# Attention's values taken for 512 queries at once, and VectorE's sorting put ahead of its wait for stores, in a two-layer diffusion backbone

## The chip, the cores and the metric

The kernel runs on one core of one Trainium2 chip, as one program. The metric is the device time of one execution in microseconds; of several executions the median counts. Profiles show one execution each.

## The reference, cut to what matters

A latent stream of 512 tokens and a context of 256 tokens, both 1024 wide, pass two layers. Layer 0 mixes with a bidirectional gated recurrence, layer 1 with latent attention of 16 heads; behind each stands a mixture of 16 experts, where each expert chooses its tokens. All in float32. What the change touches:

```
def attend(q, k, v):                      # 512 queries, 768 keys (latent + context), 16 heads
    s = jnp.einsum('bqhd,bkhd->bhqk', q, k).astype(jnp.float32) * ATTN_SCALE
    p = jax.nn.softmax(s, axis=-1).astype(v.dtype)
    return jnp.einsum('bhqk,bkhd->bqhd', p, v)

def ec_moe(h, router, w_up, w_down):
    cap = CAPACITY_FACTOR * T // N_EXPERTS               # 64 of 512 tokens, 32 of 256
    aff = jax.nn.softmax((h @ router).astype(jnp.float32), axis=-1)
    gate, idx = lax.top_k(jnp.swapaxes(aff, 1, 2), cap)
    xg = h[bidx, idx]
    up = jnp.einsum('becd,edf->becf', xg, w_up)
    hid = jax.nn.silu(up[..., :D_EXPERT]) * up[..., D_EXPERT:]
    y = jnp.einsum('becf,efd->becd', hid, w_down) * gate[..., None].astype(h.dtype)
    return jnp.zeros_like(h).at[bidx, idx].add(y)
```

A head has 96 numbers for query and key and 64 for the value. An expert's weights are 12 MB (8 chunks of `up`, 4 of `down`, 1 MB each); each layer reads 192 chunks.

## The kernel before, in words

The program is written engine by engine, with semaphores by hand; each engine runs its instructions in the order of the text. SP issues the loads of weights in the order of one list (`chunks`, L415) into buffers of 1 MB: `ring`, slots 0 to 7, and `ring_x`, slots 8 to 18, which lie over memory that the mixers use before. Each load waits until its slot is free (`used[slot]`, counted up by the last matmul that reads it, or by VectorE where a whole area is handed over), so one load that waits holds all later ones. `free_at` holds planning numbers that choose the slot of each chunk.

**Choosing tokens** (`choose`, L1404, VectorE; `turn_choice`, L638, TensorE). VectorE makes the affinities, TensorE turns them, VectorE takes 64 places in 8 rounds of maximum, index and replacement (L1425 to L1428), TensorE turns the lists, VectorE forms the indices `idx_t` and releases GpSimd's first gather (L1737). Between affinities and sorting stands `open_experts` (L1381): it waits until the rows of `stream` and `normed` have been stored, fills `mod_a`, `mod_b` and a zero area, and marks slots of `ring_x` as free. `residual_norm` and GpSimd's `stores` run ahead of it.

**Attention** (L817, L1150, L1582, L1767) runs in a loop of 4 groups of 4 heads. A group starts with projections: `kv_project` for 6 tiles of 128 tokens, with `turn_keys`, then `q_project` for 4 tiles with `turn_queries`; VectorE splits each result in two parts. Then come 16 units of one head and 128 queries, by pairs of heads, and in a pair by query tile. For unit u the engines do:

- TensorE: `scores(u)` into one half of `wide` (needs the exponential of u - 2), then `turn_probs(u - 3)` into `turned`; after every second unit `values(w)` for the pair of units before, into `duo`.
- VectorE: reciprocal of u - 1 (L1634, needs its exponential), maximum of u (L1638), its share of copying turned probabilities of u - 3 to `PT` (L1646).
- ScalarE: its share of that copy (L1168), then the exponential (L1176, needs the maximum) into `prob`, which has `LAG` = 3 places.
- GpSimd: probabilities times reciprocal (L1770).

`values(w)` is 12 calls, each with 64 columns of `V` as the stationary operand and 128 queries as the moving one; two heads go to the two halves of the partitions. `PT` holds two pairs of units, so its copies wait for the `values` of two pairs earlier (`s_av`). At a pair's end VectorE copies 512 queries from `duo` to `OT`. The float32 matmuls stand in the profile as two records each.

**After attention** `out_project` (L577) applies `w_o`; five small turnings ahead of it mark the slots of `uq` and `ukv` free. The weights of attention lie in `ring`: `mla_in` 0 to 2, `uq` 3 to 5, `ukv` 6 and 7, `w_o` 0 to 3. Slots 15 to 18 (`EARLY`) are marked free at the end of attention.

## Time and profile before

| | us |
|---|---|
| median of 3 runs | 1939.77 (1939.23 to 1940.5) |
| profiled execution | 1941.09, its span 1939.4 |
| TensorE busy (matmuls) | 1678.6, 87% of the span |
| VectorE, ScalarE, GpSimd busy | 623.4, 487.6, 202.4 |
| DMA | 528.6 MB, mean 273 GB/s |
| layer 0's experts | 409.7 to about 960 |
| attention's groups | scores of the first from 1079.5; ends at 1126.5, 1198.0, 1269.1, 1341.5: 71.5 each |
| first expert's matmuls of layer 1 | 1440.07; first of its buffers reloaded at 1443.8 |
| first gather, layer 0 and layer 1, until it has landed | 8.5 and 6.3 |
| TensorE's clock under 1 in attention | 1080 to 1090, 1158 to 1161.5, 1295 to 1305 |

The span is that of one execution on the chip; the profiled execution's own time is 1.7 us longer. Engine times are sums of instructions, so a busy TensorE says nothing of its pace: the clock (PEclk) is 1 at 2.4 GHz and 0.5 at 1.2 GHz. The chain of waits, followed back from the last instruction, gives 61% of the span to TensorE and 20% to SP's queue of weight loads (L415).

### The profile page before, as it was taken

Reading aid. Unit: us, or ns where it says so; the run is one execution under the profiler, and the core shown is the slowest. Engines: PE = TensorE matmul, PEld = TensorE weight load, DVE = VectorE, ACT = ScalarE, POOL = GpSimd, SP = SyncE. Lnnn points to the kernel's source line nnn. Section 1 sums busy time; section 2 is a strip of 40 time slices with the busy share of each in tenths; the row PEclk is TensorE's granted clock in tenths of the full one; section 3 lists DMA queues with packets and bytes.
Section 4 is the critical chain, followed back from the end, with each engine's and each line's share of the span. In section 5 each row is a group of like instructions: output and inputs, shape, how many; then the busy total and the mean of one; then the engine's idle time right before and its main releaser. Section 6 shows DMA issues by size and latency. Waiting matters only on the chain.

```text
span 1939.4 us, 22466 instructions
## 1 busy us (share of the span) xinstructions
PE 1678.6 (87%) x9117; PEld 787.8 (41%) x9117; DVE 623.4 (32%) x1333; ACT 487.6 (25%) x847; POOL 202.4 (10%) x199
## 2 busy tenths in 40 slices
PE   4999979759999999999969989899949978787874
PEld 2677634323333333333245767767423322222221
DVE  4666643321121222212134555553341111111111
ACT  5678741201110111111141434533210000000001
POOL 1000010000000000000000323413000000000000
PEclk8999989879999999999979899989959999999997
DMA  9454451799999999999741000002579999999997
GB/s 363 161 194 155 174 201 70 274 399 355 390 402 385 402 380 402 397 389 373 247 178 66 1 1 0 0 0 116 213 288 404 398 397 413 399 413 397 413 397 294
DMA packets 92082, 528.59 MB, mean 273 GB/s; under 512 B 11875, under 2 KB 20176, under 8 KB 36448
## 3 DMA queue, kind: packets, MB, share of 16 engines
q1 hardware_dynamic: 80704, 489.84, 63.0%
q0 software_dynamic: 11296, 37.58, 7.2%
q8 instruction: 61, 1.00, 0.2%
q14 instruction: 21, 0.17, 0.0%
HBM read 504.21 MB, written 23.17 MB: 272 GB/s over the span
## 4 chain that ended last, share of the span: by engine, by line
PE 61%; SPq 20%; ACT 6%; DVE 5%; DMA 5%; issue 2%; DVEq 0%; ACTq 0%; POOLq 0%
SPq L415 20%; PE wide L680 14%; PE wide L593 7%; PE duo L720 6%; PE wide L688 6%; PE turned L465 6%; PE wide L538 5%; PE duo L730 3%; PE wide L881 2%; PE duo L904 2%; PE duo L826 2%; DMA sb_ring_x<-moe_w_down 1%; DMA sb_ring<-ada_w 1%; PE duo L845 1%; PE wide L791 1%
## 5 line engine op out<-in xcount | busy, mean ns | idle before, releaser
L680 PE MATMUL wide<-sb_ring_x,sb_xT 128*64 128x512 f32 x1136 | 267.4, 612 | 39.6 <-DMA sb_ring_x<-moe_w_up 38.6
L680 PE MATMUL wide<-sb_ring,sb_xT 128*64 128x512 f32 x912 | 213.0, 609 | 27.9 <-DMA sb_ring<-moe_w_up 26.2
L1466 DVE TENSOR_TENSOR sb_hid<-wide,sb_sg 128x512 f32<-128x512 f32 x32 | 22.1, 691 | 617.7 <-ACT sb_sg L1091 312.7
L1091 ACT ACTIVATE sb_sg<-wide 128x512 f32<-128x512 f32 x32 | 19.1, 598 | 674.9 <-PE wide L688 346.4
L680 PEld LDWEIGHTS wide<-sb_ring_x,sb_xT 128*64 128x64 f32 x1136 | 77.2, 140 | 215.7 <-issue 134.9
L720 PE MATMUL duo<-sb_ring_x,sb_hidT 128*64 128x512 f32 x592 | 138.5, 601 | 9.1 <-DMA sb_ring_x<-moe_w_down 9.0
L1758 POOL DMA_INDIRECT stream<-sb_ye,sb_idx_t x30 | 43.1, 1436 | 901.8 <-DVE sb_ye L1489 901.8
L680 PEld LDWEIGHTS wide<-sb_ring,sb_xT 128*64 128x64 f32 x912 | 62.6, 139 | 165.3 <-issue 109.3
L1770 POOL TENSOR_TENSOR sb_prob<-sb_prob,sb_asum 128x768 f32<-128x768 f32 x64 | 93.9, 1466 | 260.6 <-DVE sb_asum L1634 260.6
L593 PE MATMUL wide<-sb_ring,sb_areaY 128*128 128x512 f32 x192 | 85.5, 605 | 9.7 <-DVE sb_areaY L1365 9.7
L720 PE MATMUL duo<-sb_ring,sb_hidT 128*64 128x512 f32 x368 | 86.2, 601 | 6.0 <-DMA sb_ring<-moe_w_down 5.4
L1481 DVE SCALAR_TENSOR_TENSOR sb_ye<-duo,sb_gate_t,sb_gffn 64x512 f32<-64x512 f32 x30 | 22.3, 743 | 204.2 <-PE duo L730 103.7
L1111 ACT ACTIVATE sb_ye<-duo 64x512 f32<-64x512 f32 x30 | 17.8, 594 | 271.3 <-PE duo L730 146.9
L720 PEld LDWEIGHTS duo<-sb_ring_x,sb_hidT 128*64 128x64 f32 x592 | 38.2, 136 | 95.9 <-issue 67.2
L538 PE MATMUL wide<-sb_hT_hi,sb_w_hi 128*128 128x512 f32 (+1 forms) x256 | 70.1, 356 | 6.7 <-DVE sb_hT_lo L1304 6.7
L538 PE MATMUL wide<-sb_hT_lo,sb_w_hi 128*128 128x512 f32 (+1 forms) x256 | 67.4, 345 | 0.0
L538 PE MATMUL wide<-sb_hT_hi,sb_w_lo 128*128 128x512 f32 (+1 forms) x256 | 66.8, 343 | 0.0
L688 PE MATMUL wide<-sb_ring_x,sb_xT 128*32 128x512 f32 x568 | 65.6, 595 | 0.0
L1176 ACT ACTIVATE sb_prob<-wide,sb_asum 128x768 f32<-128x768 f32 x64 | 57.7, 901 | 30.5 <-DVE sb_asum L1638 30.4
L1638 DVE TENSOR_REDUCE sb_asum<-wide 128x1 f32<-128x768 f32 x64 | 60.7, 948 | 13.7 <-PE wide L882 13.6
L593 PEld LDWEIGHTS wide<-sb_ring,sb_areaY 128*128 128x128 f32 x192 | 37.0, 195 | 54.8 <-issue 44.9
L465 PE MATMUL turned<-sb_ident,sb_prob 128*128 128x128 f32 x384 | 54.9, 280 | 5.1 <-ACT sb_PT L1168 5.1
(302 smaller groups left out, 2388.3 us busy)
## 6 DMA issues: line engine op xcount, KB each, us to landing
sb_ring_x<-moe_w_up SPq DMA_DIRECT2D x142, 1024.0 KB, 13.0
sb_ring<-moe_w_up SPq DMA_DIRECT2D x114, 1024.0 KB, 14.3
sb_ring_x<-moe_w_down SPq DMA_DIRECT2D x80, 1024.0 KB, 15.9
sb_ring<-moe_w_down SPq DMA_DIRECT2D x48, 1024.0 KB, 13.2
sb_ring<-ada_w SPq DMA_DIRECT2D x40, 1024.0 KB, 6.7
sb_ring<-lru_w_in SPq DMA_DIRECT2D x8, 1024.0 KB, 9.1
sb_ring_x<-ada_w SPq DMA_DIRECT2D x8, 1024.0 KB, 7.8
sb_ring<-lru_w_out SPq DMA_DIRECT2D x4, 1024.0 KB, 6.5
```

The costliest lines, as they stand in the source:

```text
L415: sp.dma_start(dst, src).then_inc(landed[slot], 16)
L465: return nc.tensor.transpose(dst, src, ident[0:n, 0:n])
L538: ins = mm(wide[:, b, :] if i == 0 else wide[:, b + 1, 0:TC], w[:, p % 2, k, :], seg(h[:, k, :], i), start=k == 0 and n == 0, stop=k == KD ...
L593: ins = mm(wide[:, b + n, :], lhs(k, t), w[:, n * BANK:(n + 1) * BANK], start=k == 0, stop=k == KD - 1)
L680: ins = mm(wide[n * CAPL:(n + 1) * CAPL, s, :], xT[:, k, 0:CAPL], w[:, at:at + BANK], start=k == 0, stop=k == KD - 1)
L688: ins = mm(wide[n * CAPC:(n + 1) * CAPC, 2, :], xT[:, k, CAPL:M], w[:, n * BANK:(n + 1) * BANK], start=k == 0, stop=k == KD - 1)
L720: ins = mm(lat[n * CAPL:(n + 1) * CAPL, :], hidT[:, 2 * (c % 2) + r, h * CAPL:(h + 1) * CAPL], w[:, r, n * BANK:(n + 1) * BANK], start=c = ...
L730: ins = mm(both[at:at + CAPC, :], hidT_c[:, 2 * (c % 2) + r, h * CAPC:(h + 1) * CAPC], w[:, r, n * BANK:(n + 1) * BANK], start=c == 0, sto ...
L1176: fn(prob[:, u % LAG, :], wide[:, b:b + 2, :].rearrange("p a n -> p (a n)")[:, 0:T], ACT.Exp, bias=asum[:, 0, u % 4:u % 4 + 1], accum_out= ...
L1638: v.tensor_reduce(asum[:, 0, u % 4:u % 4 + 1], wide[:, b:b + 2, :].rearrange("p a n -> p (a n)")[:, 0:T], AX_X, ALU.max, negate=True).then ...
L1758: pool.indirect_dma_start(out=stream, out_offset=bass.IndirectOffsetOnAxis(ap=idx_t[0:M, e:e + 1], axis=0), in_=(ye if e < E - 1 else xg)[ ...
L1770: g_.tensor_tensor(prob[:, u % LAG, :], prob[:, u % LAG, :], asum[:, 2, u % 4:u % 4 + 1].to_broadcast([P, T]), ALU.mult).then_inc(s_pn, 1)
```

## The change

1. `values(pair)` takes 512 queries of two heads in one call, twice in a group: after turning unit 8, and after the last unit. Units go head by head. The turned probabilities of a whole head are kept: head number modulo 3 picks one of three places, two in slots 0 to 2 of `ring`, the third in `PT`, now [128, 6, 512]. A copy waits on `s_av` at the first unit of a head only.
2. The four loops over groups are written out, with constants in the waits. The next group's first `kv_project` stands ahead of a group's last `values`.
3. `w_o` lies in slots 6, 7, 3 and 4; `uq` and `ukv` are freed by matmuls of the last group; slots 0 to 2 are opened with `EARLY`. The five small turnings are gone.
4. The waits for stores and the marks move into the sorting (`open_buffers`; after round 4 in layer 0, after round 1 in layer 1); the fills of `open_experts` move behind the release of the first gather. TensorE gets a wait for them ahead of layer 1's first rows.

```
+    W_O = (6, 7, 3, 4)
+    PT_SLOTS = (0, 1, 2)
     for j in range(4):
-        chunk(("w_o", j), j)
+        chunk(("w_o", j), W_O[j])
     opened(range(RING, NCH))
+    opened(PT_SLOTS)
     for slot in range(NCH):
-        free_at[slot] = now + (2 if slot < 4 else 1 if slot < RING else 0 if slot in EARLY else 3)
+        free_at[slot] = now + (1 if slot in EARLY or slot in PT_SLOTS else 2 if slot in W_O else 3 if slot >= RING else 0)
...
-            ("prob", [P, LAG, T], F32), ("PT", [P, 2, 2, TT, P], F32), ("asum", [P, 3, 8], F32))
+            ("prob", [P, LAG, T], F32), ("PT", [P, TT, TL], F32), ("asum", [P, 3, 8], F32))
...
+        def turned_probs(head):
+
+            if head % 3 == 2:
+                return PT[:]
+            two = ring[:, 0:3, :].rearrange("p a b -> p (a b)")
+            return two[:, head % 3 * TT * TL:(head % 3 + 1) * TT * TL].rearrange("p (k n) -> p k n", k=TT)
...
+                if lay == 1:
+                    pe.wait_ge(s_ye[1], 1)
                 turn_rows(0, None)
...
-            with pe.Fori(0, NG) as g:
+            for g in range(NG):
...
-                kv_project(0)
+                if g == 0:
+                    kv_project(g, 0)
...
-                def values(w):
-
-                    pe.wait_ge(s_PTa, g * 16 + (2 * w + 3))
-                    pe.wait_ge(s_PTd, g * 16 + (2 * w + 3))
-                    _, t, pair, _ = unit(2 * w)
+                def values(pair):
+
+                    pe.wait_ge(s_PTa, g * 16 + (8 * pair + 9))
+                    pe.wait_ge(s_PTd, g * 16 + (8 * pair + 9))
                     for k in range(TT):
                         for hh in range(2):
-                            ins = mm(duo[hh * VD:(hh + 1) * VD, pair, t * P:(t + 1) * P], V[:, k, 2 * pair + hh, :],
-                                     PT[:, w % 2, hh, k, :], start=k == 0, stop=k == TT - 1)
+                            h = 2 * pair + hh
+                            ins = mm(duo[hh * VD:(hh + 1) * VD, pair, :], V[:, k, h, :], turned_probs(HG * g + h)[:, k, :],
+                                     start=k == 0, stop=k == TT - 1)
                     ins.then_inc(s_av, 1)
...
                         turn_probs(u - LAG)
-                        if (u - LAG) % 2 and u - LAG >= 3:
-                            values((u - LAG) // 2 - 1)
-                values(U // 2 - 1)
+                        if u - LAG == 2 * TLT:
+                            values(0)
+                if g + 1 < NG:
+                    kv_project(g + 1, 0)
+                values(1)
...
-            for n, name in enumerate([("uq", j) for j in range(KQ)] + [("ukv", j) for j in range(KKV)]):
-                turn(duo[0:32, 1, 32 * n:32 * n + 32], ident[0:32, 0:32]).then_inc(used[place[name][0]], 1)
...
-                        w, hh = divmod(u - LAG, 2)
+                        h, t = divmod(u - LAG, TLT)
                         act.wait_ge(s_ptr, g * 32 + (2 * (u - LAG) + 1))
-                        if hh == 0 and w >= 2:
-
-                            act.wait_ge(s_av, g * 8 + (w - 1))
+                        if t == 0 and HG * g + h >= 3:
+
+                            act.wait_ge(s_av, (HG * g + h - 3) // 2 + 1)
...
-            def open_experts(lay):
-
-                M, s = CAP[lay], 2 * lay + 1
+            def open_buffers(lay):
 
                 dve.wait_ge(s_st[lay], 16 * FFT[lay])
                 dve.wait_ge(s_nst[lay], 16 * FFT[lay])
+                for j in range(RING, NCH):
+                    if lay == 0 or j not in EARLY:
+                        mark(used[j], 1)
+
+            def open_experts(lay):
+
+                M, s = CAP[lay], 2 * lay + 1
...
-                open_experts(lay)
                 dve.wait_ge(s_afft, lay + 1)
...
+                    if r == (CAPL // 16 - 1 if lay == 0 else 0):
+                        open_buffers(lay)
...
                 mark(s_sel, 1)
+                open_experts(lay)
...
-            for j in EARLY:
+            for j in PT_SLOTS + EARLY:
                 mark(used[j], 1)
```

VectorE in `choose(0)`, before. `sb_aff` are the affinities, `sb_marks` the marks that open slots, `sb_affT` the turned affinities.

```order
L1418 TENSOR_TENSOR sb_aff<-sb_aff,sb_mx 128x2x16 x3
L1392 COPY sb_mod_a<-sb_cols 128x8x64
L1392 COPY sb_mod_b<-sb_cols 128x8x64
L1392 COPY sb_mod_a<-sb_cols 128x8x32
L1392 COPY sb_mod_b<-sb_cols 128x8x32
L1395 MEMSET sb_hid_c 64x512
L1195 MEMSET sb_marks 128x1 x12
L1422 COPY sb_affT<-turned 48x256
```

The same place after, and under it the middle of the sorting.

```order
L1436 TENSOR_TENSOR sb_aff<-sb_aff,sb_mx 128x2x16 x3
L1439 COPY sb_affT<-turned 48x256
L1442 MAX sb_lists<-sb_affT 48x8
L1443 MAX_INDEX sb_top_i<-sb_lists,sb_affT 48x8
L1445 MATCH_REPLACE sb_affT<-sb_lists,sb_affT 48x256
```

```order
L1442 MAX sb_lists<-sb_affT 48x8
L1443 MAX_INDEX sb_top_i<-sb_lists,sb_affT 48x8
L1445 MATCH_REPLACE sb_affT<-sb_lists,sb_affT 48x256
L1211 MEMSET sb_marks 128x1 x11
L1442 MAX sb_lists<-sb_affT 48x8
L1443 MAX_INDEX sb_top_i<-sb_lists,sb_affT 48x8
```

The four copies and the zeroing are gone from ahead of the sorting, and the marks, whose first waits for the stores, stand behind the fourth round.

TensorE at the end of a group, before: the scores of unit 15 and what follows them. `sb_prob` are probabilities to be turned, `sb_V` the values, L817 the loop's own end.

```order
L882 MATMUL wide<-sb_k_hi,sb_q_lo 128x256
L465 MATMUL turned<-sb_ident,sb_prob 128x128 x12
L904 MATMUL duo<-sb_PT,sb_V 64x128 x12
L465 MATMUL turned<-sb_ident,sb_prob 128x128 x12
L904 MATMUL duo<-sb_PT,sb_V 64x128 x12
L899 REGISTER_ALU
L904 MATMUL duo<-sb_PT,sb_V 64x128 x12
L817 REGISTER_ALU
L817 COMPARE_AND_BRANCH
```

The end of the second group, after.

```order
L898 MATMUL wide<-sb_k_hi,sb_q_lo 128x256
L470 MATMUL turned<-sb_ident,sb_prob 128x128 x24
L833 MATMUL duo<-sb_ring,sb_ckvT 128x512 x2
L920 MATMUL duo<-sb_ring,sb_V 64x512 x12
L833 MATMUL duo<-sb_ring,sb_ckvT 128x512 x2
L470 MATMUL turned<-sb_ident,sb_ktok 96x128 x4
L833 MATMUL duo<-sb_ring,sb_ckvT 128x512 x2
L470 MATMUL turned<-sb_ident,sb_ktok 96x128 x4
```

The three last `values` of 128 queries have become one of 512, the four turnings stand alone behind the scores, and the next group's first projection (L833) has moved ahead of `values`.

TensorE in the middle of a group, before: a turning with the `values` behind it, and the next unit.

```order
L465 MATMUL turned<-sb_ident,sb_prob 128x128 x6
L904 MATMUL duo<-sb_PT,sb_V 64x128 x12
L876 REGISTER_ALU
L881 MATMUL wide<-sb_k_hi,sb_q_hi 128x512
L882 MATMUL wide<-sb_k_hi,sb_q_hi 128x256
L881 MATMUL wide<-sb_k_lo,sb_q_hi 128x512
L882 MATMUL wide<-sb_k_lo,sb_q_hi 128x256
L881 MATMUL wide<-sb_k_hi,sb_q_lo 128x512
L882 MATMUL wide<-sb_k_hi,sb_q_lo 128x256
L465 MATMUL turned<-sb_ident,sb_prob 128x128 x6
```

The same after, from the unit ahead of `values(0)`.

```order
L898 MATMUL wide<-sb_k_hi,sb_q_lo 128x256
L470 MATMUL turned<-sb_ident,sb_prob 128x128 x6
L920 MATMUL duo<-sb_ring,sb_V 64x512 x12
L897 MATMUL wide<-sb_k_hi,sb_q_hi 128x512
L898 MATMUL wide<-sb_k_hi,sb_q_hi 128x256
L897 MATMUL wide<-sb_k_lo,sb_q_hi 128x512
L898 MATMUL wide<-sb_k_lo,sb_q_hi 128x256
L897 MATMUL wide<-sb_k_hi,sb_q_lo 128x512
L898 MATMUL wide<-sb_k_hi,sb_q_lo 128x256
L470 MATMUL turned<-sb_ident,sb_prob 128x128 x6
```

`values` stands once between two units, with four times the columns, and no longer behind every second one.

## Rows read from the trace of the kernel before

**Rows 1.** The page: two lines of 40 equal slices of the span, busy tenths.

```profile
PE   4999979759999999999969989899949978787874
...
DMA  9454451799999999999741000002579999999997
```

**Rows 2.** The chain of waits: start, length (us), engine, tile, line, count of records.

```profile
1242.42 1.46 PE duo L904 x24
...
1273.13 1.72 PE duo L826 x4
...
1475.27 7.02 PE duo L720 x32
```

**Rows 3.** Instructions in order of time, third group: start, us, instruction [idle <-releaser].

```profile
1231.10 0.94 DVE L1638 TENSOR_REDUCE sb_asum<-wide 128x1 f32<-128x768 f32 x1
...
1232.15 0.90 ACT L1176 ACTIVATE sb_prob<-wide,sb_asum 128x768 f32<-128x768 f32 x1 [0.68 <-DVE sb_asum L1638]
...
1233.17 0.16 DVE L1634 RECIPROCAL sb_asum<-sb_asum 128x1 f32<-128x1 f32 x1 [0.80 <-ACT sb_prob L1176]
...
1233.19 0.50 PE L881 MATMUL wide<-sb_k_hi,sb_q_hi 96*128 96x512 f32 x1 [0.17 <-ACT sb_prob L1176]
1233.25 0.94 DVE L1638 TENSOR_REDUCE sb_asum<-wide 128x1 f32<-128x768 f32 x1
```

**Rows 4.** The same view, later in that group.

```profile
1243.81 0.50 PE L881 MATMUL wide<-sb_k_hi,sb_q_hi 96*128 96x512 f32 x1
...
1245.18 0.96 DVE L1638 TENSOR_REDUCE sb_asum<-wide 128x1 f32<-128x768 f32 x1 [0.67 <-PE wide L882]
...
1250.26 0.96 DVE L1638 TENSOR_REDUCE sb_asum<-wide 128x1 f32<-128x768 f32 x1 [0.67 <-PE wide L882]
```

**Rows 5.** The same view, start and end of that group.

```profile
1224.83 0.94 DVE L1638 TENSOR_REDUCE sb_asum<-wide 128x1 f32<-128x768 f32 x1
...
1261.51 0.90 ACT L1176 ACTIVATE sb_prob<-wide,sb_asum 128x768 f32<-128x768 f32 x1
...
1266.22 2.84 PE L904 MATMUL duo<-sb_PT,sb_V 128*64 128x128 f32 x48
...
1269.23 0.69 DVE L1627 COPY sb_OT<-duo 128x512 f32 x1 [2.48 <-PE duo L904]
...
1272.53 0.60 PE L465 MATMUL turned<-sb_ident,sb_ktok 128*96 128x128 f32 x4
```

**Rows 6.** Stretches: start:end, length, busy PE, PEld, DVE, ACT, POOL, PEclk, DMA share, GB/s.

```profile
438.00:442.00 4.00, 3.67 (x14) 2.26 (x16) 0.18 (x1) 0.87 (x2) 0.00 (x0) 0.57 1.04 357
...
1080.00:1090.00 10.00, 9.85 (x33) 7.95 (x32) 5.31 (x9) 4.63 (x10) 4.40 (x3) 0.50 0.00 1
...
1224.00:1270.00 46.00, 42.31 (x385) 35.71 (x384) 24.34 (x51) 26.12 (x50) 23.46 (x16) 1.00 0.00 0
```

**Rows 7.** Instructions in order of time, where layer 0 chooses its tokens.

```profile
374.28 0.40 PE L465 MATMUL turned<-sb_ident,sb_aff 128*48 128x128 f32 x2 [0.35 <-DVE sb_aff L1418]
380.88 0.43 DVE L1392 COPY sb_mod_a<-sb_cols 128x512 f32<-128x512 f32 x1 [6.66 <-DMA normed<-sb_units]
...
382.83 0.42 DVE L1422 COPY sb_affT<-turned 48x256 f32<-48x256 f32 x1
...
384.77 0.42 DVE L1425 MAX8 sb_lists<-sb_affT 48x8 f32<-48x256 f32 x1
...
397.89 0.98 POOL L1737 DMA_INDIRECT sb_xg<-normed,sb_idx_t  x1 [15.43 <-DVE sb_marks L1195]
```

**Rows 8.** Waits of TensorE from 420 to 960 us: us in total, times, longest.

```profile
PE turned L465 <- DVE sb_xT L1461: 4.3, 1, 4.3
```

**Rows 9.** Layer 1's choice, in order of time; below, one stretch as in rows 6.

```profile
1414.10 0.62 PE L465 MATMUL turned<-sb_ident,sb_aff 128*48 128x128 f32 x2 [1.91 <-DVE sb_aff L1418]
...
1416.03 0.42 DVE L1422 COPY sb_affT<-turned 48x256 f32<-48x256 f32 x1
...
1436.00:1440.00 4.00, 1.97 (x8) 1.56 (x8) 1.65 (x4) 0.00 (x0) 0.63 (x1) 0.50 0.02 3
```

More of the change, by code:

```diff
@@ L826, in kv_project @@
                         ins = mm(duo[:, t % 2, :], ckvT[:, k, t * P:(t + 1) * P],
-                                 ring_at(("ukv", k))[:, bass.ds(g * BANK, BANK)], start=k == 0, stop=k == KKV - 1)
+                                 ring_at(("ukv", k))[:, g * BANK:(g + 1) * BANK], start=k == 0, stop=k == KKV - 1)
+                        if g == NG - 1 and t == TT - 1 and k == 0:
+                            ins.then_inc(used[place["ukv", 0][0]], 1)
                     ins.then_inc(s_kv, 1)
@@ L870, in scores @@
                 def scores(u):
[L871 removed]
+                    h, t = divmod(u, TLT)
                     if h == 0:
@@ L1149, in _ @@
                 fn(mx[:, 3, t:t + 1], mx[:, 1, t:t + 1], ACT.Sqrt, bias=eps[:, 0:1], scale=1.0 / KVL).then_inc(s_mzs, 1)
-            with act.Fori(0, NG) as g:
+            for g in range(NG):
                 for t in range(TT):
@@ L1399, in open_experts @@
                 mark(s_ye[lay], 1)
-                for j in range(RING, NCH):
-                    if lay == 0 or j not in EARLY:
-                        mark(used[j], 1)
             def choose(lay):
@@ L1581, in _ @@
             loop_chain = Chain(dve, s_dloop)
-            with dve.Fori(0, NG) as g:
+            for g in range(NG):
                 loop_chain.n = g * TLT
@@ L1766, in _ @@
             pool.dma_start(ropes[:], rope.rearrange("(t p) i f -> p t i f", p=P)).then_inc(s_rope, 16)
-            with pool.Fori(0, NG) as g:
+            for g in range(NG):
                 for u in range(HG * TLT):
```

34 lines of the change are left out of this document (18 added, 16 removed).

## The prediction, made before the changed kernel ran

> **What bounds the kernel now.** I read the page's slices first. TensorE is at 7 to 9 tenths almost everywhere, but the DMA line splits the run in three: full DMA and full TensorE through layer 0's experts (slices 9 to 19), no DMA at all through attention (slices 23 to 27), full DMA and a TensorE at 7 to 8 tenths in layer 1's experts at the end [rows 1]. So a microsecond counts differently by stage.
>
> Layer 0's experts are TensorE's: from 420 to 960 us TensorE's one wait over 1 us was for VectorE, 4.3 us, and none was for a DMA [rows 8]. What starts them sooner ends them sooner. Layer 1's experts wait for weights, but their first weights do not: all 19 buffers are full and the DMA engines idle (share 0.02) from 1436 to 1440 us, waiting for the first expert's matmuls to free a buffer [rows 9]. So the last stage too begins where TensorE begins it, and every shift before it comes out whole.
>
> Attention is a row of 4 groups of 16 units (one head, 128 queries). In a unit TensorE computes scores, VectorE their maximum, ScalarE the exponentials, VectorE the reciprocal, GpSimd the product, and TensorE turns the probabilities of three units earlier. Two limits show. In the middle of a group, maxima stand 5.08 us apart for two units, VectorE idle behind TensorE for 0.67 us [rows 4]: that is TensorE's limit, two units of scores and turning and one `values` of 1.46 us [rows 2]. At a group's start there is no `values`, and then another limit shows: maximum at 1231.10, exponential at 1232.15, reciprocal at 1233.17, next maximum at 1233.25 [rows 3]. VectorE does not start a maximum before the reciprocal of the unit before, so VectorE and ScalarE take turns, 2.15 us for each unit, whatever TensorE does. That chain lies only 0.39 us a unit under today's 2.54.
>
> **The change, part by part.**
>
> (a) `values` for 512 queries. Before, a pair of heads takes 4 calls of 24 records with 128 columns: 4 x 1.46 = 5.84 us, and a gap of about 0.17 us ahead of each. After it is one call of 24 records with 512 columns. The trace has that shape in the expert's `down`: 32 records in 7.02 us, 0.219 each [rows 2], so 24 take 5.27 us. TensorE saves 0.57 us and three gaps for each of 8 pairs: about 1.1 us each, 9 in all. But where it is spent decides. TensorE's work a unit without `values` is (5.08 - 1.46 - 0.17) / 2 = 1.72 us, less than the chain's 2.15. So the loop runs at 2.15 a unit, and the 5.27 us come as one lump in the middle and one at the end.
>
> The Trainium skill ("TensorE: Matmul & The Clock Gate", Part 1, "Wait — 56ns, not 53.3ns?") gives each matmul a fixed cost of about 2.5 ns on top of its columns. The rows show more here: 60.8 ns for a record of 128 columns against 219 / 4 = 54.9, so 8 ns for each of three records saved. By the page's figure the eight pairs would save 1.4 us of matmul time in place of 4.6. Neither reaches the end of the kernel if the chain sets the pace.
>
> Middle of a group, counted from its first maximum (`wide` has two halves, so scores of unit u start 1.04 us after the exponential of unit u - 2 [rows 3]): maximum 11 at 11 x 2.15 = 23.5 (the first steps are a little shorter); maximum 9 at 19.2, its exponential at 20.25, scores 11 at 21.3, then turning, `values(0)` from 23.2 to 28.4. Scores 12 start there, and their maximum comes 1.37 later, as in [rows 4]: 29.8 instead of 25.7. The stall is 4.1 us. Three more units and 1.05 give exponential 15 at 37.3. Before, that is 1261.51 - 1224.83 = 36.7 [rows 5]. So all that the loop won (about 3.5 us) and the saved gaps are spent by one stall: **+0.6 us a group**.
>
> End of a group. Before: from exponential 15 to the end of the last two `values`, which take 2.84 us, 1269.06 - 1261.51 = 7.55 us [rows 5]. After: the last turning starts about 3.4 us after exponential 15 (nearly as now: GpSimd's product and ScalarE's copies of units 13 to 15 set it) and takes 0.57; then `kv_project` of the next group, 1.72 [rows 2], covering the wait for the last copies; then 5.27: 10.96. That is +3.4 us, of which the next group gets something back: before, its first key turning starts 3.47 us after the end of `values` [rows 5]; after, the second projection waits for the copy to `OT` (0.17 + 0.69 + 0.05 us) and takes 1.72, so 2.6: -0.8. The last group has no projection to cover: +2.4. Sum over the groups: 4 x 0.65 + 3 x (3.4 - 0.8) + 2.4 = **+12.8, with rounding 13 us**. Bounds: the stall may be 1 us shorter or longer in each group, so 9 to 17.
>
> (b) Loops written out. The waits of the loops compare with registers; written out they compare with constants. Nothing in the trace prices that alone. A wait of one semaphore inside the loop releases its instruction in 0.03 us, as outside; the exponential that waits for two comes 0.11 us after its maximum ends (1231.10 + 0.94 to 1232.15). If the second wait gets free, 0.08 us for 52 units is 4.2 us; if not, 0. A loss is possible through instruction fetching, but the DMA engines are idle there, so 0.5 at most. I take **-1** (range -4.2 to +0.5), nearer to nothing since a second wait stays.
>
> (c) TensorE's clock. The third group ran at full clock throughout; the first lost it from 1080 to 1090 us [rows 6] (the fourth for as long, the second for some 3 us: the table of the profile), right after a stretch in which TensorE only turned queries and idled. In layer 0, five microseconds of idling and turning, 433 to 438, were followed by 438 to 442 at clock 0.57 [rows 6]. After the change each group ends with about 6 us (from scores 15 to the next matmul that isn't a turning) where TensorE turns four times 0.57 us and idles between; now it is 2.3 us. I expect 1.2 GHz there in about three of four groups, over some 3.4 us of dense matmuls as in layer 0, which costs half of it, 1.7 us: **+5** (range 0 to 14: no dip, or twice that length in every group).
>
> (d) VectorE sorts first in layer 0. TensorE has turned the affinities at 374.68, and VectorE waits 6.66 us for the stores, fills `mod_a`, `mod_b` and `hid_c`, and copies `affT` at 382.83 [rows 7]. After, the copy starts at about 374.75. A round takes 384.77 - 382.83 - 0.45 = 1.49 us, so four are done at 381.2; the stores had landed at 380.88, so the wait is then free, and the 11 marks cost 0.25. The choice, and the gather at 397.89, come 8.08 - 0.25 = 7.8 us earlier. The filling (1.8 us) now runs behind the gather, which takes 8.5 us (table); `ada_read(4)` and its turning move back by 1.8 us and still end under it. SP's 11 loads of `ring_x` are let go at 381.3 instead of 382.7. **-7.8 us** (-5.5 if the gather, now deeper inside the burst of weight loads, takes 2 us longer; -8.5).
>
> (e) The same in layer 1. No store was waited for there; the fills stood between the turned affinities (1414.72) and the copy at 1416.03 [rows 9]: -1.3, and 7 marks inside the sorting +0.15: **-1.1**. TensorE's new wait for `s_ye` has nothing queued that could go, and the fills (1.9 us) lie under a gather of 6.3 us (table).
>
> (f) Slots. `w_o` sits in 6, 7, 3, 4 and loads while the last group runs, one expert chunk (slot 5) too, seven more at the end of attention; before it was w_o's last chunk and eight. Then SP waits in order for slots 3, 4, 6, 7: three of those loads start up to 16 us later than now. They fit: 3 x 2.6 us more before the last seven, whose end moves to about 1436.5 on the old scale, while the first buffer is freed at 1443.8 now (table) and at 1442.7 with (e). Idle DMA from 1436 to 1440 [rows 9] is the cover; if it were gone, up to 3 us. Counted 0. The five small turnings ahead of `out_project` go: **-0.3**.
>
> Sum: +12.8 - 1 + 5 - 7.8 - 1.1 - 0.3 = +7.6 us by the middles; with the rounding of (a) up, **+8**. The profiled execution took 1941.1 us (span 1939.4), 1.3 over the median of 1939.8; against the median I forecast **1948**.
>
> **The rivals.**
>
> *The clock holds.* All as above without (c): 1939.8 + 3 = 1942.8, +-2. For it: two of four groups come through their present idle stretch undisturbed or nearly. Against it: that stretch gets twice as long.
>
> *Not slower: the lump costs nothing in the middle.* If the stall of 4.1 us were covered in each group, 16.4 us go: 1948 - 16.4 = 1931.6. It decides at a stall of about 2 us, that is if VectorE and ScalarE had two units in hand when `values(0)` starts. Against it: scores start only 1.04 us after an exponential [rows 3], so they have under two. A stronger reading, that TensorE is the bound and its saved 9 us come out whole, gives 1939.8 - 9 - 9.2 = 1921.6; [rows 3] speak against it.
>
> *The clock oscillates in the loop.* At 1.2 GHz TensorE needs 9.85 of 10 us for what it does at a slower pace [rows 6]; a unit then takes about 3.0 us in place of 2.15, so each stretch of 10 us costs some 3 us; one or two more of them in each group but those that have one: about +8, 1956. The Trainium skill says the same of kernels that cycle PSUM banks ("TensorE: Matmul & The Clock Gate", "A second HAM failure mode: psum-queue depth-cycling"): idling briefly between groups of matmuls, often enough, makes the clock swing. Against it: the starts of groups, which already run chain-bound for 10 us, kept full clock in two groups of four or lost it for 3 us only.
>
> *Layer 0 gives nothing back.* If weights, not TensorE, set layer 0's experts, (d) is lost: 1955.8. [rows 8] speak against it, though the DMA share is as full there [rows 1].
>
> **How the numbers follow.** A difference under 0.2% (3.9 us) is about what a measurement of this kernel can't tell from none. Forecast (1944 to 1953): 0.50, slower. Clock holds: 0.25, of it 0.08 slower and 0.17 within. Lump covered, or TensorE the bound: 0.10, faster. Clock oscillates: 0.10, slower. Layer 0's gain lost: 0.05, slower. So faster 0.10, within 0.17, slower 0.73. The range leaves out the faster case and the outer half of the slow ones and takes in the bounds of (a) to (d) about their middles: 1939 to 1957.
>
> **What would show it.** `values` at 24 records in 5.3 us. Maxima 2.1 to 2.2 us apart through most of a group and one step of 6.3 us after unit 11. About 11 us from a group's last exponential to the end of its `values`; groups of 74 to 76 us where they are 71.5 now. Clock 0.5 inside `kv_project` and `values(1)`. Layer 0's gather at about 390, its experts 7.8 us earlier up to 960. DMA idle just ahead of layer 1's first expert. I am wrong if the 6.3 us step isn't there, or if the loop's pace is well under 2.1 us (then (b) was too small), or if layer 0's experts end no sooner.

## The result, and the profile after

The changed kernel took **1945.4 us** (median of 14, 1943.4 to 1949.0) against 1940.95 (14 runs) for the kernel before on the same chip: ratio 1.0023 (1.0015 to 1.0031), some 4.5 us slower. The forecast was 1948, slower. The executions of one kernel spread over some 6 to 8 us here; the profiled one of after is the slowest of its 14 (1949.0, span 1947.3), that of before is at its median. So totals are compared by the ratios, and the traces by stage.

| stage, us | before | after | difference | forecast |
|---|---|---|---|---|
| start to affinities turned, layer 0 | 374.28 | 375.20 | +0.9 | 0 |
| from there to the first gather | 23.61 | 15.75 | -7.9 | -7.8 |
| gather to VectorE's first copy of projected keys, where attention begins | 658.06 | 659.32 | +1.3 | 0 |
| from there to the last copy to `OT` | 285.69 | 297.69 | +12.0 | +16.8 |
| last copy to `OT` to the end of the span | 597.76 | 599.34 | +1.6 | -1.4 |

Attention holds the loss, as forecast, though less. The chain of waits of after, in the first group and at the end of the last (start, length, engine, tile, line, count):

```profile
1097.99 5.30 PE duo L920 x24
...
1104.58 0.97 DVE sb_asum L1658
...
1115.68 1.72 PE duo L833 x4
1117.40 5.33 PE duo L920 x24
...
1340.96 6.98 PE duo L920 x24
```

`values(0)` takes 5.30 us and is followed by scores and a maximum; at the end `kv_project` and `values(1)` stand in a row on the chain. In the last group `values(1)` takes 6.98 us, at a clock that had fallen (below). VectorE's instructions around the middle lump, in order of time:

```profile
1098.13 0.94 DVE L1658 TENSOR_REDUCE sb_asum<-wide 128x1 f32<-128x768 f32 x1
...
1104.58 0.96 DVE L1658 TENSOR_REDUCE sb_asum<-wide 128x1 f32<-128x768 f32 x1 [4.28 <-PE wide L898]
...
1122.75 0.69 DVE L1647 COPY sb_OT<-duo 128x512 f32<-128x512 f32 x1 [6.60 <-PE duo L920]
```

One step of 6.45 us, VectorE idle for 4.28 of it, where [rows 4] have two units in 5.08. All other maxima stand 2.08 apart, but for one step of 2.6 near the start of each of the last three groups. The last row answers to the copy in [rows 5]: VectorE waits 6.60 us for it, 2.48 before. Stretches at the ends of the four groups (columns as in [rows 6]):

```profile
1113.00:1121.00 8.00, 7.01 (x34) 3.27 (x36) 1.17 (x3) 1.48 (x3) 1.47 (x1) 1.00 0.00 0
1186.00:1194.00 8.00, 6.81 (x26) 3.94 (x28) 1.33 (x4) 2.25 (x5) 1.70 (x2) 0.79 0.01 2
1262.00:1270.00 8.00, 7.48 (x30) 4.09 (x32) 0.90 (x3) 1.22 (x3) 1.28 (x1) 0.79 0.01 2
1338.00:1346.00 8.00, 7.04 (x25) 2.98 (x25) 0.85 (x2) 1.20 (x2) 0.28 (x1) 0.61 0.00 0
```

The granted clock (third number from the end) falls in the ends of the last three groups, not of the first. From the last maximum to the copy to `OT` it takes 11.92, 13.13, 13.13 and 13.39 us; before, 8.80 in all four.

Layer 0's choice, the rows that answer to [rows 7]:

```profile
375.64 0.42 DVE L1439 COPY sb_affT<-turned 48x256 f32<-48x256 f32 x1 [0.50 <-PE turned L470]
...
382.08 0.24 DVE L1211 MEMSET sb_marks<- 128x1 f32 x10
...
390.95 1.24 POOL L1757 DMA_INDIRECT sb_xg<-normed,sb_idx_t  x1 [7.51 <-DVE sb_marks L1211]
```

The sort starts at once, and the wait for stores inside it costs under 0.1 us. From 420 to 960 us TensorE waits just as in [rows 8] (4.3 us, once). In layer 1 the stretch of [rows 9] looks otherwise. First the gather, from the chain of waits (6.33 us before), then two stretches:

```profile
1435.56 8.85 DMA sb_xg<-normed,sb_idx_t
```

```profile
1436.00:1440.00 4.00, 0.00 (x0) 0.00 (x0) 0.99 (x3) 0.00 (x0) 0.52 (x1) 0.50 1.01 422
...
1444.00:1448.00 4.00, 2.48 (x10) 1.86 (x12) 1.67 (x4) 0.00 (x0) 1.24 (x2) 0.50 0.07 29
```

The DMA engines are full while the gather runs, and idle only from 1444 on.

### The profile page after: what moved, and what is told of

Its sections match the earlier page's. It is cut to its first block, busy times and chain, and to the rows that moved or that the text cites. A ratio compares the mean times of both kernels' runs of the same rounds, so it can differ in the third digit from the quotient of the medians.

```text
span 1947.3 us, 20675 instructions
## 1 busy us (share of the span) xinstructions
PE 1683.1 (86%) x8536; PEld 758.4 (39%) x8536; DVE 620.8 (32%) x1336; ACT 481.4 (25%) x844; POOL 202.5 (10%) x199
## 4 chain that ended last, share of the span: by engine, by line
PE 58%; SPq 20%; ACT 8%; DVE 7%; DMA 4%; issue 2%; ACTq 0%; DVEq 0%; POOLq 0%
SPq L420 19%; PE wide L685 14%; PE wide L598 7%; PE duo L725 6%; PE wide L693 6%; PE wide L543 5%; PE turned L470 4%; PE duo L735 3%; DVE sb_asum L1658 2%; ACT sb_prob L1192 2%; PE duo L833 2%; PE duo L920 2%; DMA sb_ring<-moe_w_down 1%; DMA sb_ring<-ada_w 1%; PE duo L854 1%
## 5 line engine op out<-in xcount | busy, mean ns | idle before, releaser
L685 PE MATMUL wide<-sb_ring_x,sb_xT 128*64 128x512 f32 x1160 | 272.8, 613 | 34.9 <-DMA sb_ring_x<-moe_w_up 34.9
L725 PE MATMUL duo<-sb_ring_x,sb_hidT 128*64 128x512 f32 x568 | 132.9, 600 | 9.5 <-DMA sb_ring_x<-moe_w_down 9.3
L1778 POOL DMA_INDIRECT stream<-sb_ye,sb_idx_t x30 | 43.1, 1436 | 901.9 <-DVE sb_ye L1509 901.9
L725 PE MATMUL duo<-sb_ring,sb_hidT 128*64 128x512 f32 x392 | 92.0, 601 | 6.2 <-DMA sb_ring<-moe_w_down 5.8
L470 PE MATMUL turned<-sb_ident,sb_prob 128*128 128x128 f32 x384 | 59.3, 293 | 8.4 <-ACT sb_ring L1184 5.8
## 6 DMA issues: line engine op xcount, KB each, us to landing
sb_ring_x<-moe_w_down SPq DMA_DIRECT2D x75, 1024.0 KB, 14.3
```

Of the source, the lines that this page charges most:

```text
L470: return nc.tensor.transpose(dst, src, ident[0:n, 0:n])
L685: ins = mm(wide[n * CAPL:(n + 1) * CAPL, s, :], xT[:, k, 0:CAPL], w[:, at:at + BANK], start=k == 0, stop=k == KD - 1)
L725: ins = mm(lat[n * CAPL:(n + 1) * CAPL, :], hidT[:, 2 * (c % 2) + r, h * CAPL:(h + 1) * CAPL], w[:, r, n * BANK:(n + 1) * BANK], start=c = ...
L1778: pool.indirect_dma_start(out=stream, out_offset=bass.IndirectOffsetOnAxis(ap=idx_t[0:M, e:e + 1], axis=0), in_=(ye if e < E - 1 else xg)[ ...
```

## The experiments

All kernels were timed beside the kernel before; traces are of one execution each.

**The two halves of the change.** The kernel before with the sorting first:

```
+                    if r == (CAPL // 16 - 1 if lay == 0 else 0):
+                        open_buffers(lay)
...
                 mark(s_sel, 1)
+                open_experts(lay)
```

> The kernel before with part 4 alone (sorting ahead of the wait for stores, fills behind the gather's release). Theory A (layer 0 is TensorE's, layer 1's first expert sets the end): layer 0's gather 7.8 us earlier and all of it kept, layer 1's first gather 1.1 us earlier with the same 6.3 us latency, since the slots are those of before: 1940.9 - 8.9 = about 1932. Rival B (some of layer 0's gain is given back by the weight loads, as the profile of the changed kernel hints, where only 5.5 of 7.9 us were left at the start of attention): -6.5, 1934.5. Rival C (it gives nothing): 1941.

Measured: 1935.5, ratio 0.9973 (0.9964 to 0.9981), some 5 us less, nearest to rival B. Trace: layer 0's gather at 389.52 (-8.4), its first expert 8.1 sooner, attention 7.2 sooner; 0.5 us of each was there before the sort. Layer 1 gives nothing: its gather is issued 1.2 us sooner after the last copy to `OT` but takes 8.63 us instead of 6.33.

The changed kernel with the sorting as before (`open_experts` with its waits and marks ahead of the sort):

> The changed kernel without part 4. Theory A: attention costs 10 to 12 us and the later slots some 2 us more: +12 to +14 against before, about 1954. Rival (the two parts do not add, for example because attention hides behind something): within 5 us of before. With the first run it tells whether the parts add up to the measured +4.4.

Measured: 1955.1, ratio 1.0072 (1.0058 to 1.0086), +14.0. Attention in the trace: 297.40 us, +11.7. So attention costs and the sorting gives back, as the prediction had it. How much is less sure: the halves timed apart add up to 14.0 - 5.2 = 8.8 us and the whole is 4.5 over before, somewhat more than the intervals allow, while the traces differ the other way (+10.9 and -8.0 against +7.9). No run explains that.

**Loops written out** in the kernel before, nothing else:

```
-            with pe.Fori(0, NG) as g:
+            for g in range(NG):
```

> The kernel before with the four group loops written out and nothing else. Theory A (waits on registers cost 0.07 us a step in the chain of VectorE and ScalarE, which binds only the first units of a group here): maxima 2.08 apart in place of 2.15 at a group's start, middle unchanged at 5.08 for two: -1 to -3 us. Rival 1 (the 0.17 us gaps around values are register arithmetic too): 16 gaps a group go, -8 to -10 us. Rival 2 (loading more instructions costs): 0 to +3.

Measured: 1940.8, ratio 1.0000 (0.9989 to 1.0010). But the pace did change: where VectorE and ScalarE set it, maxima stand 2.08 apart in place of 2.07 to 2.16, and where TensorE sets it two units still take 5.08. In a group in which the clock did not fall, the first and the last maximum are 35.48 us apart (35.61 before), and from there to the last copy to `OT` it takes 8.52 (8.80): 0.4 us a group, 1.6 in all, less than this timing resolves (2 us either way).

**Is it the lump?** The changed kernel with one of six key tiles in `values(0)`:

```
+                    tiles = range(1) if pair == 0 else range(TT)
-                    for k in range(TT):
+                    for k in tiles:
```

> The changed kernel, but values(0), in the middle of each group, runs over one of its six key tiles, 4 records in place of 24; five sixths of the weighted sum for the first two heads of each group are left out. Theory A (one lump of 5.3 us stalls VectorE and ScalarE, since they have under two units in hand): the step after unit 11, 6.45 us in the changed kernel, becomes about 2.6 (1.72 + 0.88), 3.85 less in each of four groups, so 15 us less in all, about 1930; the other steps stay at 2.08. Rival B (the lump is paid for by work that TensorE has to do anyway, and steps behind it are then longer): under 4 us less in all, 1942 or more.

Measured: 1923.4, ratio 0.9913 (0.9900 to 0.9926), 22 us under the changed kernel. VectorE's row in the middle of the first group:

```profile
1098.87 0.96 DVE L1659 TENSOR_REDUCE sb_asum<-wide 128x1 f32<-128x768 f32 x1
```

It stands 2.14 after the one before (1096.73), not the 2.6 expected: what is left of `values(0)`, 1.0 us of TensorE, hides almost wholly, and the 4.3 us taken away came out as 4.31, 17.2 in four groups. Theory A holds. The other 4 to 5 us were not expected: here the clock did not fall in any group's end (11.91 us three times, 10.86 in the last).

**The same work in small pieces.** By head:

```
-                        if u - LAG == 2 * TLT:
-                            values(0)
+                        if u >= LAG + TLT:
+                            h, t = divmod(u - LAG - TLT, TLT)
+                            values(h, ((0, 1), (2,), (3, 4), (5,))[t])
...
-                values(1)
+                values(3, range(TT))
```

> The changed kernel, but the values are computed head by head and key tile by key tile: 1 or 2 of a head's 6 tiles behind each turning of the next head's units, and only the last head's 6 tiles, 2.64 us, stand at the group's end behind the next group's kv_project. The work is the same. Theory A (the lumps, not the work, cost the time): in the middle TensorE needs 1.72 + 0.66 = 2.38 us a unit for 8 units where VectorE and ScalarE want 2.08, so the stall of 4.37 us in a group becomes 2.4; the end gets 2.6 shorter; 4 x 4.6 = 18 us less than the changed kernel, about 1927, and below the kernel before by 14. From a group's first maximum to its second copy to OT 44.8 us in place of 49.5. Rival B (small pieces between scores let TensorE's clock fall or steps of 2.16 and 2.60 us don't even out, so each piece delays a maximum by its full length): at best the end's gain, 1935 to 1940.

Measured: 1974.8, ratio 1.0175 (1.0162 to 1.0188): 30 us over the changed kernel, and neither theory's number. "The work is the same" was wrong. The chain of waits, in the second group:

```profile
1173.24 1.86 PE duo L920 x4
...
1177.02 1.00 PE duo L920 x2
```

Four records of one head take 1.86 us and two take 1.00, 0.43 each and 0.14 for the piece; 24 of two heads in turn took 5.30, 0.22 each. Two heads write different halves of the partitions of `duo`, and in turn they run at the same time, as TensorE's records in the trace of after show:

```profile
1117.33 0.64 PE L920 MATMUL duo<-sb_PT,sb_V 128*64 128x512 f32 x1
1117.34 0.64 PE L920 MATMUL duo<-sb_ring,sb_V 128*64 128x512 f32 x1
1117.81 0.59 PE L920 MATMUL duo<-sb_PT,sb_V 128*64 128x512 f32 x1
```

The records of a pair start 0.01 us apart, the next pair 0.48 later. The Trainium skill ("TensorE: Matmul & The Clock Gate", Part 3: Packing small matmuls) says that matmuls whose outputs lie in different column groups run concurrently; the rows agree, here with two halves of 64. So this run doubled TensorE's time for the values, some 10 us a group, of which 7 reached the end, and it says nothing on lumps. The next one keeps heads in turn, with blocks of two heads and 256 queries:

```
+                    for k in tiles:
+                        for hh in range(2):
+                            ins = mm(duo[hh * VD:(hh + 1) * VD, pair, half * 2 * P:(half + 1) * 2 * P], V[:, k, 2 * pair + hh, :],
+                                     turned_probs(HG * g + b)[:, hh, k, :], start=k == 0, stop=k == TT - 1)
```

> The changed kernel with another grain: a block is a pair of heads and 256 queries (four units, heads in turn as in the kernel before); its values are 24 records of 256 columns, the two heads' records in turn, put behind the turnings of the next block, 2, 1, 2 and 1 key tiles at a time (4 records, 0.44 us, a tile); the last block's stand at the group's end behind the next group's kv_project. Theory A (a record of one head alone takes 0.43 us and of two heads in turn 0.22 each, which spoilt the run by head; with the heads in turn spreading pays): 7 steps of 2.08 and 8 of about 2.45 in place of 35.6 us in the kernel before and 35.5 in the changed one, the end 9.5 us in place of 11.9 to 13.4 (changed) and 8.8 (before): per group 3.5 to 4.5 us less than the changed kernel and 1.6 less than the one before, so about 1930, below the run with the sorting alone (1935.5). Rival B (the small pieces cost their gaps and the clock): steps of 2.6 to 2.9 from unit 7 on, no better than the attention of before, 1935 to 1940.

Measured: 1934.75, ratio 0.9966 (0.9954 to 0.9979): 10.7 us under the changed kernel, level with the sorting alone. The lump is gone, but not for nothing; chain of waits, steps in the first group:

```profile
1086.58 1.01 PE duo L926 x8
1087.59 0.43 PE wide L902
...
1089.51 0.58 PE duo L926 x4
```

A tile's 4 records take 0.43 us and each piece 0.15 more. The first part of the scores behind a piece takes 0.43 us, where straight behind a turning it takes 0.23 (the kernel before, 1245.80). So two units take 2 x 1.92 + 1.01 + 0.58 = 5.43 us (steps of 2.50 and 2.93), more than the 5.08 of [rows 4], where the two share one piece. The end takes 10.95 us, not 9.5. So A holds against the changed kernel, B against the one before: attention lasts 287.1 us, 285.7 before.

**The clock.** Two matmuls of 512 columns whose result is not used, behind the turnings of units 12 to 14 (first run), or one of 256 (second run, shown):

```
+                        if U - 1 <= u < U + LAG - 1:
+                            pe.wait_ge(s_OT, g * 2 + 3)
+                            mm(duo[:, 0, 0:TC], ident[:], ckvT[:, 0, 0:TC], start=True, stop=True)
```

> The changed kernel with two idle-filling matmuls of 512 columns (0.88 us together; their result is not used) behind each of the turnings of units 12 to 14, where TensorE otherwise waits. Theory A (TensorE's clock falls because a group's end is mostly idle): clock 1.00 through kv_project and values(1); from the last maximum to the second copy to OT 11.9 us in place of 13.1 to 13.4 in the last three groups, and the first five steps of groups 2 to 4 at 2.08 in place of 2.18: about 1.7 us a group, 5 in all, 1940.5. Rival B (the fall has another cause): the same dips, and no gain, or up to 3 us more where a fill runs into the next turning.

Measured: 1952.4, ratio 1.0056 (1.0043 to 1.0069), 7 us over the changed kernel. The clock was 1.00 in all four ends, but each fill took 1.8 us, not 0.88 (two records a matmul, 0.45 each), and 14.3 us for an end is more than the dip had cost. One of its six executions took 4129.9 us; nothing here explains it.

> The changed kernel with one idle-filling matmul of 256 columns (0.44 us by the trace of the earlier fill, where each record of 512 columns took 0.45; its result is not used) behind each of the turnings of units 12 to 14, where TensorE waits 0.56 to 0.85 us. The heavier fill held the clock at 1.00 in every group's end but each of its three fills took 1.8 us. Theory A (the idle end is what lets the clock fall, and a small fill holds it): last maximum to second copy to OT 12.0 us in all four groups, against 11.9, 13.1, 13.1 and 13.4, and the first five steps of the groups at 2.08: about 5 us less than the changed kernel, 1940.5. Rival B (so small a fill doesn't hold it, or the fills push the turnings back): within 2 us of the changed kernel's 1945.4.

Measured: 1941.5, ratio 1.0000 (0.9991 to 1.0010), 4 us under the changed kernel, near theory A. The trace at the ends of groups two and four, to set beside the rows above:

```profile
1188.00:1196.00 8.00, 7.21 (x29) 2.31 (x28) 1.39 (x5) 0.16 (x1) 0.00 (x0) 1.00 0.00 0
...
1334.00:1342.00 8.00, 6.61 (x31) 2.79 (x32) 1.17 (x9) 0.60 (x1) 0.00 (x0) 1.00 0.00 0
```

Clock 1.00, the ends 11.92, 11.91, 11.92 and 10.87 us. So the falls at the ends cost 1.2 + 1.2 + 2.5 = 4.9 us in the changed kernel. The dips of 0.5 us at the start of two groups stayed. The runs by head and with blocks of 256 queries, which have pieces of `values` behind those turnings, kept 1.00 in their ends too. But that an idle end alone lets the clock fall is not shown: the run with the short `values(0)` had the same idle ends without a fall, and with attention alone the second end had none while the first did.

**Layer 1.** Another order of `w_o`'s slots, so that fewer loads start late:

```
-    W_O = (6, 7, 3, 4)
+    W_O = (3, 4, 6, 7)
```

> The changed kernel with w_o in slots 3, 4, 6, 7 in place of 6, 7, 3, 4, so that SP waits for the slots in the order in which out_project frees them. Theory A (the weight loads behind w_o come late, still run when layer 1's first gather is issued, and make it last 8.9 us in place of 6.3): the gather is back at 6.3 to 6.8 us, time 2 to 2.6 us under the changed kernel, 1943. Rival (the gather's latency is chance or comes from elsewhere): no change, 1945.4.

Measured: 1947.1, ratio 1.0025 (1.0014 to 1.0036), no gain. The slots' four loads were now issued from 1396 to 1413 (1403 to 1414 before this edit), and the DMA engines had a pause ahead of `ring_x`'s loads, yet the gather took 8.46 us. So it is not those loads alone that it waits for. What is left is the burst that VectorE opens itself: 7 loads, which before began 14.7 us ahead of the gather, and with part 4 only 12.7. That lead is not all either: with the lead of 14.7 us the gather took 6.33 us before, and in the runs with the loops out and with attention alone

```profile
1430.21 7.25 DMA sb_xg<-normed,sb_idx_t
1441.95 8.18 DMA sb_xg<-normed,sb_idx_t
```

With the lead of 12.7 it took 7.93 to 8.91 in nine kernels. To tell what the burst is worth, the marks in layer 1 behind everything:

```
                 open_experts(lay)
+                if lay == 1:
+                    for j in range(RING, NCH):
+                        if j not in EARLY:
+                            mark(used[j], 1)
```

> The kernel before with the sort first in layer 0 (as in the run with the sorting alone), but in layer 1 the buffers of ring_x are opened only behind the choice, about 14 us later, so that the gather meets idle DMA engines. Theory A (layer 1's experts begin where TensorE begins, as the prediction had it, and their loads have room): the gather takes some 2.5 us in place of 8.6, the first expert starts 6 us sooner, and the kernel ends up to 6 us sooner than the run with the sorting alone (1935.5), about 1930. Rival B (from the opening on layer 1 is set by the bytes of its weights: from the last copy to OT to the last store it took 577.2 to 577.4 us in four kernels whose first expert started at different times): the first expert starts 6 us sooner all the same, but the loads 14 us later, of which 4 to 5 us were idle before: about 9 us more, 1944.

Measured: 1941.1, ratio 1.0000 (0.9991 to 1.0009): 5.6 us over the sorting alone, 8.6 in the traces. The gather, in the chain of waits, and stretches of this run:

```profile
1422.17 3.81 DMA sb_xg<-normed,sb_idx_t
```

```profile
1410.00:1422.00 12.00, 0.53 (x4) 0.34 (x4) 10.51 (x42) 0.00 (x0) 0.00 (x0) 0.50 0.00 0
...
1426.00:1430.00 4.00, 2.91 (x12) 1.92 (x14) 1.67 (x4) 0.00 (x0) 1.52 (x2) 0.50 0.99 401
```

Issued on idle DMA engines the gather takes 3.81 us, and the first expert starts 5 us sooner. The kernel ends later all the same. TensorE's waits for the weights of `up`, of this run and then of the sorting alone (us, times, longest):

```profile
PE wide L680 <- DMA sb_ring_x<-moe_w_up: 38.0, 39, 2.9
PE wide L680 <- DMA sb_ring<-moe_w_up: 29.4, 29, 2.7
```

```profile
PE wide L680 <- DMA sb_ring_x<-moe_w_up: 35.6, 36, 2.8
PE wide L680 <- DMA sb_ring<-moe_w_up: 26.2, 29, 2.8
```

So theory B holds in its direction: layer 1's end follows its loads, not its first expert. Opening them 14.5 us later cost 8.8 us of this stage. And in the twelve kernels of this document (before and after among them) that open them 73.8 to 75.2 us after the last copy to `OT`, it took 596.0 to 599.3 us from that copy to the end, though the first expert began from 98.4 to 100.0 us after it; the one in which it began first, before, ended 1.8 us later than the earliest.

**Towards a faster kernel.** Attention of before with the loops out, the next group's first `kv_project` ahead of the last values, and the sorting first:

```
+                if g + 1 < NG:
+                    kv_project(0, g + 1)
                 values(U // 2 - 1)
```

> The attention of the kernel before (values for 128 queries), loops written out, the next group's first kv_project moved ahead of a group's last values, and the sorting first. Theory A: against the run with the sorting alone (1935.5) the move is neutral or a small gain: kv_project (1.72 us) covers the wait for the last copies (0.9) and saves 0.9 at the next group's start, so 0 to -0.9 in each of three groups, 1933 to 1935.5. Rival B (the later copy to OT and values delayed by kv_project cost their full length): up to 3 us more, 1938.

Measured: 1934.9, ratio 0.9968 (0.9956 to 0.9980), within theory A's range. The trace goes against its reason. The second copy to `OT` of the first group, and two stretches, the start of the first group and nearly all of attention:

```profile
1122.16 0.69 DVE L1636 COPY sb_OT<-duo 128x512 f32<-128x512 f32 x1 [4.42 <-PE duo L907]
```

```profile
1074.00:1084.00 10.00, 7.58 (x45) 6.21 (x46) 5.04 (x10) 6.00 (x10) 4.40 (x3) 1.00 0.00 1
1074.00:1340.00 266.00, 241.39 (x1817) 182.93 (x1818) 146.24 (x374) 118.27 (x224) 93.85 (x64) 1.00 0.01 4
```

An end takes 10.58 us, 8.52 with the loops out alone, and the next start only 0.9 less: the move costs 1.2 us in each of three groups, as rival B has it. Yet attention lasts 284.4 us, as with the loops out alone (284.1), because the clock was 1.00 from the first group to the last, where with the loops out it fell in two groups at a cost of 3.2 us. The next run, with the same attention, kept 1.00 throughout too (284.4). Whether the move is what holds the clock was not tested apart.

The same, with `ring_x` opened earlier in layer 1:

```
+                if lay == 1:
+                    open_buffers(lay)
                 dve.wait_ge(s_afft, lay + 1)
```

> The run with the moved kv_project and the sorting first, but in layer 1 VectorE opens ring_x before it waits for the turned affinities, where the kernel before opened it (there behind the fills), and not behind the first round of the sort; that is some 2.5 us sooner against the choice. Theory A (layer 1's end goes with the start of its loads, since opening 14 us later cost 8.6 us of span although the first expert began 5 us sooner): the gather, behind the same loads, takes about 6 us in place of 8.6, and the kernel ends 2 to 2.5 us sooner, 1932 to 1933; from the opening's first load to the last scatter 502 to 503.5 us as in five kernels. Rival B (the opening has slack of the 4 to 5 us in which the DMA engines idle ahead of the first expert): no change, 1934.9.

Measured: 1934.6, ratio 0.9963 (0.9948 to 0.9978): not told apart from the run before it. The trace goes theory A's way in the end, though not in the gather: gather 7.45 us where 6 was expected, from the last copy to `OT` to the end 594.7 in place of 597.6, from the opening's first load to the last scatter 502.9 (503.0 in the run before it). One trace against an equal median: left open.

Four kernels lie at 1934.6 to 1935.5, about 6 us under the kernel before and 10 under the changed one. What they share is the sorting first, no lump of 512 queries, and `ring_x` opened ahead of the choice (the run that opened it behind has the first two as well, and took 1941.1).

## Why the prediction was right, and where its steps were off

The sign and the mechanism held: time went where VectorE and ScalarE take turns, and the values stood as lumps on the chain. Step by step:

**(a), values for 512 queries: +12.8 forecast; with (b) +11.8 forecast, 8.6 measured.** The lump is 24 records in 5.30 us (5.27 forecast), the step behind it 6.45 (6.3), from the last exponential to the end of `values(1)` 10.9 (10.96), the next start 0.9 shorter (0.8). The term that was mis-sized is the middle, by the pace of the loop: 2.15 forecast, 2.08 measured. Over 14 steps that is 1 us a group. So an undisturbed group needs 22.85 + 6.45 + 6.25 = 35.55 us from first to last maximum, and the kernel before 25.43 + 2.18 + 8.00 = 35.6: the middle costs nothing, not +0.65. One reading of the rows was wrong, without weight in the sum: the 8 ns for each record saved are mostly not the records'. With 0.15 us off for each piece (from the blocks of 256), two records in turn take (1.46 - 0.15) / 12 = 0.109 us with 128 columns and (5.30 - 0.15) / 12 = 0.429 with 512, so four of the first cost 0.008 us more than one of the second; what TensorE saves comes from three pieces fewer. The ends: 3 x (3.12 - 0.88) + 2.07 = 8.8, less 0.2 from the middles. The ends were forecast at 10.2; against the loops written out alone, whose end is 8.52, they cost 3 x (3.40 - 0.86) + 2.35 = 10.0, so their size was right and the rest is (b)'s. The run with the short `values(0)` showed that the stall is real and whole; but the faster loop had won as much as the stall took, more than I had reckoned.

**(b), loops written out: -1 forecast.** 0 in the kernel before, timed; 4 x 0.4 = 1.6 by the traces of undisturbed groups. In the changed kernel it would be the 0.07 us a step above, some 4 us, the end of its range (-4.2) that I had set aside because "a second wait stays"; that is worked out from the two paces, no run has the changed attention in loops. What a wait costs depends on who sets the pace: in the changed loop VectorE and ScalarE set it in 14 of 15 steps, before in some six.

**(c), TensorE's clock: +5 forecast.** The falls came at three of four ends, as forecast, and cost 4.9 us (the light fills gave that back), and dips of 0.5 us at three starts 1.5. But before had dips of its own, 1.4, 0.4, 0 and 1.3 us in the starts of its groups (against an undisturbed 35.61 us and 26.66 us ahead of it), which the forecast left in place: net 3.4. With 8.6 that is the 12.0 of the table. The loop never oscillated, although TensorE idles 0.36 us (2.08 - 1.72) in every unit: all steps are 2.08 us but the lump and one of 2.6 in each of three groups. What the Trainium skill ("TensorE: Matmul & The Clock Gate", "A second HAM failure mode: psum-queue depth-cycling") says of brief idling between groups of matmuls, the page named beside that rival, did not show in this loop.

**(d), sorting first in layer 0: -7.8 forecast.** -7.9 at the gather. Of it 6.6 were left when attention began (6.7 in the run with the sorting alone); some 0.6 went in the first expert, where TensorE began at 1.2 GHz and the full clock came back some 6.0 us after its start, 4.7 before. Where the other 0.6 went is not traced. Timed, the sorting gives 3.7 to 7.0 us in the kernel before; between the changed kernel with and without it the ratios differ by 9.5 us.

**(e), the same in layer 1: -1.1 forecast, 0 or worse measured.** This step failed by its reason: "the last stage too begins where TensorE begins it, and every shift before it comes out whole". Idle DMA engines from 1436 to 1440 did not mean that loads had slack. They had run out of free buffers, but in the 480 us that follow, loads are what TensorE waits for, so their start counts and the first expert's does not. The gather sits behind the burst, which the change itself opens 2 us later against it, and takes 8.85 us in place of 6.33; how much of that the later opening costs is open, since the old lead went with 6.33 to 8.18.

**(f), slots: 0 forecast, 0 found.** The other order of slots changed nothing. The cover that I named, idle DMA from 1436 to 1440, was gone in the trace (share 1.01), without the 3 us, since the loads behind it set that stage. The small turnings gave their 0.3 (from the copy to `OT` to `out_project` 0.75 us, 1.06 before).

Together by the traces: 8.6 + 3.4 - 6.6 + 0 = +5.4 where +7.6, rounded to 8, was forecast, and 4.5 is measured. That the sum came so near is partly luck: attention cost 4.8 us less than forecast, and (d) to (f) gave 2.6 less. The last stage's +1.6 in this execution, and +0.9 before the change can act, are put down to that execution: the same code of that stage took 597.6 and 596.9 in the two runs with fills, against 599.3. What the rival "the clock holds" (1942.8) describes is near what the run with the light fills shows (1941.5).

## What to carry to other kernels

A larger tile saves TensorE's time only where TensorE sets the pace; where other engines do, the saved time turns into a lump that they wait for, and it comes out whole once it is longer than what they have in hand (here 1.0 us hid, 5.3 did not). Before splitting matmuls of 64 output columns, look whether two of them run in turn at the same time. And idle DMA engines just ahead of a stage are no proof of slack: if the stage waits for loads later on, opening their buffers late costs even where the stage begins sooner (8.8 us here). Whether opening them earlier gains was left open.

## What the runs showed of the hardware that was not expected

- Records of two heads, 64 output columns each, in turn: 0.22 us a record of 512 columns; of one head alone 0.43, as long as a record with 128 output columns (`kv_project`, 4 in 1.72 us).
- Each separate piece of matmuls between turnings and scores cost 0.15 us beside its records, and 0.20 more in the first part of the scores behind it (0.43 us in place of 0.23).
- 0.44 us of matmuls in each of three gaps of 0.6 to 0.8 us went with a clock of 1.00 through four group ends, three of which had 0.61 to 0.79 without them (in one run without them all four had 1.00).
- The same gather of layer 1 took 3.81 us when issued on idle DMA engines and 6.33 to 8.91 behind seven weight loads of 1 MB.
